# Up products of a gated FFN: high and low tokens in one matmul of 512 columns, VectorE's accumulations in a new order, the product of gates and values on GpSimd

## What is computed

```python
def conv_ffn(h, up, conv_w, conv_b, down):
    hid = causal_dwconv(h @ up.astype(h.dtype), conv_w, conv_b)
    gate, val = jnp.split(hid, 2, axis=-1)
    return (jax.nn.gelu(gate) * val) @ down.astype(h.dtype)
...
        h = rms_norm(x, pre_ffn_norm[l])
        y = conv_ffn(h, ffn_up[l], ffn_conv_w[l], ffn_conv_b[l], ffn_down[l])
        x = x + rms_norm(y, post_ffn_norm[l])
```

## Time and profile before

| what | us |
|---|---|
| median of 3 runs | 2645.5 |
| lowest and highest | 2642.3, 2646.19 |
| the profiled execution's own time | 2643.04 |
| its span (first to last instruction) | 2641.2 |
| busy in the span: TensorE, VectorE, ScalarE, GpSimd | 2618.2, 1825.4, 1136.7, 362.5 |

### The profile page before, as it was taken

How to read it: one execution, slowest core, us unless ns; L and a number is a source line. 1 busy time by engine, 2 the same in 40 slices (tenths; PEclk the granted TensorE clock), 3 DMA queues, 4 the chain that set the end, 5 groups by cost and what they waited for, 6 DMA issues and landing times. The chain is left out here.

```text
span 2641.2 us, 39524 instructions
## 1 busy us (share of the span) xinstructions
PE 2618.2 (99%) x17064; PEld 2282.8 (86%) x17064; DVE 1825.4 (69%) x1816; ACT 1136.7 (43%) x1183; POOL 362.5 (14%) x358
## 2 busy tenths in 40 slices
PE   9999999999999999999999999999999999999999
PEld 8778877887888888788889999999999998877788
DVE  6556567774454666532897777877877787788886
ACT  5335245642432243422464443444444446444436
POOL 1003100260000000011010000000000022334303
PEclk9999999999999999999999999999999999999999
DMA  6225411452222221142458777777778778888863
GB/s 234 88 85 194 136 65 64 159 181 81 95 102 95 81 80 66 50 159 96 158 146 224 198 188 203 193 193 208 189 194 205 186 227 236 237 246 222 233 183 128
DMA packets 119499, 416.70 MB, mean 158 GB/s; under 512 B 8208, under 2 KB 72848, under 8 KB 80544
## 3 DMA queue, kind: packets, MB, share of 16 engines
q1 hardware_dynamic: 94800, 271.76, 29.3%
q0 software_dynamic: 24240, 142.16, 23.9%
q10 hardware_dynamic: 288, 0.27, 0.0%
HBM read 378.51 MB, written 32.51 MB: 156 GB/s over the span
## 5 line engine op out<-in xcount | busy, mean ns | idle before, releaser
L1008 PE MATMUL ps<-h_hi,w_hi 128*128 128x512 f32 x1200 | 481.6, 401 | 0.0
L1010 PE MATMUL ps<-h_hi,w_lo 128*128 128x512 f32 x1200 | 468.1, 390 | 0.0
L1009 PE MATMUL ps<-h_lo,w_hi 128*128 128x512 f32 x1200 | 467.8, 390 | 0.0
L2666 DVE TENSOR_TENSOR w_lo<-raw,w_hi 128x2048 fp32r<-128x2048 f32 x105 | 246.3, 2345 | 197.0 <-ACT w_hi L1884 196.9
L1760 PE MATMUL ps<-h_hi,w_hi 128*128 128x256 f32 x1280 | 363.2, 284 | 3.1 <-DVE w_lo L3560 3.1
L1762 PE MATMUL ps<-h_hi,w_lo 128*128 128x256 f32 x1280 | 363.0, 284 | 0.0
L1761 PE MATMUL ps<-h_lo,w_hi 128*128 128x256 f32 x1280 | 362.9, 284 | 0.0
L1884 ACT ACTIVATE w_hi<-raw 128x2048 fp32r<-128x2048 f32 x105 | 200.6, 1911 | 362.9 <-PE ps L1010 310.9
L3560 DVE TENSOR_TENSOR w_lo<-raw,w_hi 128x2048 fp32r<-128x2048 f32 x91 | 225.3, 2476 | 140.0 <-ACT w_hi L2418 139.8
L2418 ACT ACTIVATE w_hi<-raw 128x2048 fp32r<-128x2048 f32 x91 | 174.5, 1918 | 293.5 <-PE ps L1762 199.5
L1008 PEld LDWEIGHTS ps<-h_hi,w_hi 128*128 128x128 f32 x1200 | 225.3, 188 | 57.5 <-issue 11.2
(11 more groups left out here) (567 smaller groups left out, 5542.5 us busy)
## 6 DMA issues: line engine op xcount, KB each, us to landing
raw<-weights SPq DMA_DIRECT2D x142, 1024.0 KB, 4.8
raw<-weights POOLq DMA_DIRECT2D x60, 1024.0 KB, 8.3
X<-weights SPq DMA_DIRECT2D x59, 1024.0 KB, 6.6
q_raw<-weights SPq DMA_DIRECT2D x30, 1024.0 KB, 5.5
q_raw<-weights POOLq DMA_DIRECT2D x30, 1024.0 KB, 7.9
f_spill<-f_val POOLq DMA_DIRECT2D x22, 512.0 KB, 5.7
x_spill<-X POOLq DMA_DIRECT2D x8, 1024.0 KB, 8.8
f_even<-f_spill SPq DMA_DIRECT2D x6, 1024.0 KB, 8.2
```

Source lines behind the costliest of these rows:

```text
L1008: pe.matmul(o, w_hi[:, s % 2, w], h_hi[:, t, :], start=(t == 0), stop=False)
L1009: pe.matmul(o, w_hi[:, s % 2, w], h_lo[:, t, :], start=False, stop=False)
L1010: mm = pe.matmul(o, w_lo[:, s % 2, w], h_hi[:, t, :], start=False, stop=(t == 15))
L2666: V.tensor_tensor(w_lo[:, slot, :], raw[:, slot, :], w_hi[:, slot, :].bitcast(F32), ALU.subtract).then_inc(w_ready, 1)
```

## The change

- **TensorE**: `h_hi` and `h_lo`, `t1_hi` and `t1_lo`, `t3_hi` and `t3_lo` are each one tensor with the parts side by side (`h_both`, `t1_both`, `t3_both`). A high weight block is multiplied with 256 high and 256 low tokens in one matmul of 512 columns into a whole bank: the first half holds weights high x tokens high, the second weights high x tokens low. The low weight block is multiplied with the 256 high tokens as before, into the first half. A product is 32 matmuls instead of 48.
- **VectorE and ScalarE**: both halves of each product have to be added. There are 14 steps in an up quad (`E_Y5` to `E_C12`) instead of seven. ScalarE copies the first halves of S1 (into `rstd_k`, as `y5`) and A11; VectorE adds the rest. The end of the values' sum stands ahead of the low part of S1, where its last step stood behind it.
- **GpSimd** makes the product of gates and values in quads 1 to 20; VectorE makes it in quad 0 as before. The addition of a form of the tokens in quad 0 goes from GpSimd to VectorE.
- **rstd**: since `rstd_k` is used by the sums, rstd is stored to memory before the FFN and brought back after the up quads. SyncE's first load waits for that store. VectorE makes the reciprocals in quad 21, and GpSimd scales the 16 tiles of x in the quads 22 to 29 instead of 21 to 28.

```diff
-        h_hi = top.take("h_hi", [128, KT, S], F32R)
-        h_lo = top.take("h_lo", [128, KT, S], F32R)
+        h_both = top.take("h_both", [128, 2, KT, S], F32R)
+        h_hi, h_lo = h_both[:, 0], h_both[:, 1]
...
-            return ps[:, b:b + 2, N1] if q < QUADS else ps[:, b:b + 2, :]
+            return ps[:, b:b + 2, :]
+
+        EVALS = 14
+        (E_Y5, E_P1, E_C11A, E_U2A, E_U2, E_U4, E_C11, E_U3A, E_U3, E_C21A, E_C21, E_C22, E_C12A, E_C12) = range(1, EVALS + 1)
+        y5 = rstd_k[:, :].rearrange("p (m c) -> p m c", m=2)
...
             sp.wait_ge(rstd_ready, 6)
+            sp.wait_ge(f_stored, F_STORED)
             load_a11(0)
...
+            pool.dma_start(x1[:, 0, :], rstd[:, :]).then_inc(sem("x_spilled"), 16)
...
-            pool.wait_ge(*form_made.at(3))
-            nc.gpsimd.tensor_tensor(X[:, 8:16, N1], X[:, 8:16, N1], X[:, 0:8, N2], ALU.add).then_inc(form_made.sem, 1)
             for q in range(QUADS):
                 sum_q(q)
                 sum_r2(q)
...
+                if q:
+                    gate(q + 1)
                 store_f(q + 1)
...
-                t = 2 * (q - QUADS - 1)
+                t = 2 * (q - QUADS - 2)
...
-                            pe.matmul(o[:, m, :], w_hi[:, n % 2, w], hi[:, k, :], start=(k == 0), stop=False)
-                            pe.matmul(o[:, m, :], w_hi[:, n % 2, w], lo[:, k, :], start=False, stop=False)
-                            mm = pe.matmul(o[:, m, :], w_lo[:, n % 2, w], hi[:, k, :], start=False, stop=(k == 7))
+                            pe.matmul(o[:, m, :].rearrange("p (f c) -> p f c", f=2), w_hi[:, n % 2, w], both[:, :, k, :],
+                                      start=(k == 0), stop=False)
+                            mm = pe.matmul(o[:, m, N1], w_lo[:, n % 2, w], both[:, 0, k, :], start=False, stop=(k == 7))
...
+            def take_high(q, j, dst):
+                act.wait_ge(w_used, at(q, j) + 2)
+                A(dst, pair(q, j)[:, :, N1], ACT.Copy).then_inc(p1_taken.sem, 1)
+
+            def take_s1(q):
+                if q:
+                    act.wait_ge(*bank_read.at(EVALS * (q - 1) + E_C22))
+                take_high(q, J_S1, y5)
...
+            def evaluate(q, n, dst, a, b, op=ALU.add):
+
                 if n > 1:
-                    dve.wait_ge(*bank_read.at(PRODUCTS * q + n - 1))
+                    dve.wait_ge(*bank_read.at(EVALS * q + n - 1))
+                V.tensor_tensor(dst, a, b, op).then_inc(bank_read.sem, 1)
+
+            def add_high(q, n, j, dst, src, op=ALU.add):
                 dve.wait_ge(w_used, at(q, j) + 2)
...
+                evaluate(q, n, dst, src, pair(q, j)[:, :, N1], op)
+
+            def add_low(q, n, j, dst, op=ALU.add):
+                evaluate(q, n, dst, dst, pair(q, j)[:, :, N2], op)
+
+            def end_val(q):
+                add_high(q, E_C21A, J_A22, hid_b[:, :, C1], hid_b[:, :, C2], ALU.subtract)
+                add_low(q, E_C21, J_A22, hid_b[:, :, C1], ALU.subtract)
+                evaluate(q, E_C22, hid_b[:, :, C2], hid_b[:, :, C2], y5)
...
-                if q == 0:
+                if q:
+                    end_val(q - 1)
+                else:
                     first_taps(0, 1, hid_b)
                 lo(at(q, J_S1), raw[:, q % 2, :])
...
                 lo(at(q, J_A12), a12_at(q))
+                dve.wait_ge(*p1_taken.at(2 * q + 1))
+                add_low(q, E_Y5, J_S1, y5)
                 if q:
                     gate_taps(q - 1)
                 else:
-                    first_taps(1, 1, hid_b)
...
+                    dve.wait_ge(*form_made.at(3))
+                    V.tensor_tensor(X[:, 8:16, N1], X[:, 8:16, N1], X[:, 0:8, N2], ALU.add).then_inc(form_made.sem, 1)
                 lo(at(q, J_S3), q_raw[:, :])
                 if q == 0:
+                    first_taps(1, 1, hid_b)
                     form_lo(X_r[:, 8:16, N1], X[:, 8:16, N1], X_r[:, 0:8, N1], 4)
-                gated(q + 1)
...
+                dve.wait_ge(*p1_taken.at(2 * q + 2))
+                add_low(q, E_P1, J_A11, hid_b[:, :, C1])
+                dve.wait_ge(sem("f_gates"), q + 2)
+                add_high(q, E_C11A, J_A12, hid[:, :, C1], hid_b[:, :, C1])
+                dve.wait_ge(*val_conved.at(q + 2))
+                add_high(q, E_U2A, J_S2, hid_b[:, :, C2], hid_b[:, :, C1])
+                add_low(q, E_U2, J_S2, hid_b[:, :, C2])
                 lo(at(q, J_A22), a22_raw)
...
+                evaluate(q, E_U4, hid[:, :, C2], hid_b[:, :, C2], y5)
+                add_low(q, E_C11, J_A12, hid[:, :, C1])
+                if q == 0:
+                    gated(q + 1)
+                add_high(q, E_U3A, J_S3, hid_b[:, :, C2], hid_b[:, :, C2])
                 lo(at(q, J_S4), raw[:, q % 2, :])
+                add_low(q, E_U3, J_S3, hid_b[:, :, C2])
```

117 lines of the change are left out of this document (58 added, 59 removed).

## The result

| | before | after |
|---|---|---|
| median | 2645.5 (7 runs, 2642.3 to 2646.63) | 2619.67 (7 runs, 2615.12 to 2630.64) |
| ratio, 95% interval | | 0.9913 (0.9901 to 0.9924) |
| profiled execution, its span | 2643.04, 2641.2 | 2628.14, 2626.2 |

The time is inside the range, 3.2 us above the forecast. But the seven times are not one group: three lie from 2628.1 to 2630.6, four from 2615.1 to 2619.7. The median is the highest time of the lower group; with one more execution in the upper one it would have been about 2628, so its nearness to the forecast is in part luck. The profiled execution is of the upper group. I ran the same kernel again to have a profile of the lower one (`again`, 2615.37, span 2613.4), and read the two side by side.

What follows compares the result with a forecast made beforehand. Steady up quads were taken as bound by TensorE's count of matmuls. Terms -27.6 - 5.3 + 3.2 + 0.5 = -29.2 us gave 2613.8 for the profiled execution, 2616.5 as median; range 2608 to 2630 for 8 in 10.

Steps and rivals of the forecast that it cites:

- TensorE's intervals: Up products: 0.227 us per 512-column matmul plus 0.120 per 256-column one; a quad takes 38.87 us for 40.32.
- the term of -27.6: TensorE's gain over the 19 steady up quads, 1.45 us each: 27.6 us.
- C: Rival, up products: two runs cost what two matmuls cost, 0.240 us; nothing gained there, about 2645 us; chance 0.05.
- D: Rival: TensorE starts anew at every moving operand's second run, 2240 times; slower, 2768 us at half of 0.11; chance 0.06.
- VectorE in the steady quads at no cost: Steady up quads: seven more accumulations cost nothing, since every low part has at least 0.8 us left.
- GpSimd's product at no cost: Steady up quads: GpSimd's product of gates and values runs beside accumulations from PSUM and costs nothing.
- Quad 0: First up quad: moving GpSimd's addition to VectorE leaves one wait of 3.4 us at A22; -5.3 us.
- The passage: From quad 19 to 20, into the down products: waits at S3, S4 and S1 total 6.6 us for 2.8; +3.2 us.
- The down stage: Reciprocals cost nothing; scaling of x starts one quad later and x_back may come 2 us later; +0.5 us (0 to 2).
- B: Rival: VectorE's new work, or the lock with GpSimd, precedes a low part in every up quad; 2623 to 2640; chance 0.15.

Runs made afterwards that it cites:

- gate_dve: Against the changed kernel, VectorE instead of GpSimd makes the product of gates and values in quads 1 to 19; measured 2617.54 and 2620.78 us.
- one_run: Changed kernel with the 512 token columns in one run, not two, in six of seven products of up quads 1 to 18; 2632.21, 2616.05, 2618.76, 2630.24 us.

## Why the prediction came out as it did

- **TensorE's intervals: right as a price, wrong as a certainty.** 0.227 + 0.120 is what a pair takes in the short rhythm, and the quad of 38.87 came as 38.83. The two members are not what I took: means of 0.232 and 0.115 in `again`, of 0.230 and 0.117 in `gate_dve`, so that the sum is right and its terms are off by what cancels; no run shows why. In the long rhythm they are 0.236 and 0.117, the pair is 0.353 and the quad 39.57: there the term of -27.6 is -14.3 (19 x 0.75). That is also my own sign for C or D, an interval over 0.235, though the split operand that C and D blame costs nothing (`one_run`). My step had no case in which one program has two values. By the Trainium skill (TensorE: Matmul & The Clock Gate, "Wait — 56ns, not 53.3ns?") a matmul costs its columns at 2.4 GHz plus about 2.5 ns; the streams of one kind have 13 ns more than the columns (0.227 - 0.213, 0.120 - 0.107), so the trace disagrees. The merge saved 13 ns a pair in the short rhythm and 7 in the long one (0.360 less 0.347 and 0.353), for 2.5 by that rule.
- **VectorE in the steady quads at no cost: right.** No wait of TensorE in 18 quads, in either rhythm, and none when 1.15 us more stood there (`gate_dve`).
- **GpSimd's product at no cost: right**, with the accumulations beside it at 0.68 and 0.69, as the Trainium skill (SBUF — State Buffer, "Who interferes with whom") has it for VectorE instructions with one SBUF input. What I did not say is that it earns nothing either in these quads; it was worth 2.7 us at the passage in the one pair of profiles that compares it, where I had booked it as a cost.
- **Quad 0: -5.3 predicted, -4.5 measured** to S1(1) in the upper group; of the 0.8 that are missing 0.7 are the long rhythm (112 pairs at 0.353). The one wait was 3.25 at 1393.27 for 3.4 at 1392.6. In `again` it was -3.1, since the clock fell behind that wait. I had priced waits by their length alone; in the kernel before, too, the clock fell behind one.
- **The passage: mechanism right, size short by the clock.** S1(19) to S1(20) took 45.86 and 45.54 for 45.5. Over the quad of its rhythm that is 6.3 and 6.7 us of waits for 6.6, in the three places that I named: in the first profile some 1.0 at S3, 1.0 at S4 and 4.2 at S1, for 0.5, 1.6 and 4.5. S1(20) to S3(20) took 23.5 for 22.1: behind a wait of 4.27 TensorE ran at 1.2 GHz for a while. In the kernel before the wait was 1.23 and the clock stayed.
- **The down stage: +0.5 predicted, -0.7 and -1.1 measured.** The sign is wrong, and no run took this apart.
- **The rivals.** B, C and D did not happen: no low part late in the steady quads, no 0.240 + 0.120 = 0.360 a pair, no restart. Half of C is there in the long rhythm, by another cause. The profiled execution of the short rhythm, 2615.37, is 1.1 under 2616.5, that of the long one 11.6 over it. The forecast is one of two outcomes, and that the median of seven shows this one was a matter of four executions against three. (2613.8 + 2.5 is 2616.3; the 2616.5 is rounded up.)

## What to carry to other kernels

Price a merge of matmuls by the spacing in a long stream of the same mixture, not by the spacings of its members, and look at the single times of a kernel before its median: two groups are a finding. When a step is moved back on one engine, walk the queues of all that wait for it, since the wait goes to whatever stands behind the waiting instruction. In `gate_dve` three GpSimd instructions back to back were not three short delays for a VectorE instruction with two SBUF operands but one long one, so look for places where they can stand apart.
